# Two column tiles of a weight chunk on TensorE: one after the other in place of turn by turn

## What is computed

```python
h = rms_norm(x, norm_mix)
proj = h @ w_in                      # q, k, v, gates of both recurrences, merge gates
...
merged = sigmoid(ga) * (o_r @ w_ret_out) + sigmoid(gb) * (o_h @ w_hgrn_out)
x = x + merged @ w_out
g, u = split(rms_norm(x, norm_ffn) @ w_ffn_in)
x = x + (silu(g) * u) @ w_ffn_out
```

## Time and profile before

| what | value |
|---|---|
| median of three runs | 1765.47 us |
| the profiled execution | 1764.43 us, its span 1762.6 us |
| TensorE busy (matmul) | 1745.1 us, 14598 matmuls |
| VectorE, ScalarE, GpSimd busy | 1078.7, 766.9, 258.6 us |
| DMA | 334.11 MB, mean 190 GB/s |
| granted TensorE clock, mean | 0.996 of full speed |

### The profile page before, as it was taken

How to read it: one execution, slowest core, us unless ns; L and a number is a source line. 1 busy time by engine, 2 the same in 40 slices (tenths; PEclk the granted TensorE clock), 3 DMA queues, 4 the chain that set the end, 5 groups by cost and what they waited for, 6 DMA issues and landing times.

```text
span 1762.6 us, 37793 instructions
## 1 busy us (share of the span) xinstructions
PE 1745.1 (99%) x14598; PEld 1727.5 (98%) x14598; DVE 1078.7 (61%) x1290; ACT 766.9 (44%) x915; POOL 258.6 (15%) x378
## 2 busy tenths in 40 slices
PE   9899999999999999999999999999999999999997
PEld 9899999999999999999999999999999999999997
DVE  7776776766767755555566655555555555545444
ACT  7354454554554643444433444443444434333332
POOL 0561642733715000000000000000000000000000
PEclk9999999999999999999999999999999999999999
DMA  9566666676666555555566565565555655555553
GB/s 311 178 214 196 193 206 202 184 216 187 207 203 188 181 180 182 187 181 183 182 207 204 174 194 180 179 184 183 180 180 178 190 179 183 185 181 180 188 184 109
DMA packets 390169, 334.11 MB, mean 190 GB/s; under 512 B 12640, under 2 KB 387680, under 8 KB 390112
## 3 DMA queue, kind: packets, MB, share of 16 engines
q1 hardware_dynamic: 369968, 318.58, 58.6%
q10 hardware_dynamic: 20144, 14.72, 2.7%
HBM read 316.93 MB, written 16.32 MB: 189 GB/s over the span
## 4 chain that ended last, share of the span: by engine, by line
PE 97%; DVE 1%; DMA 1%; ACT 0%; issue 0%; DVEq 0%; SPq 0%; ACTq 0%
PE pA L1168 15%; PE pA L1170 15%; PE pA L1169 15%; PE pB L1168 13%; PE pB L1170 13%; PE pB L1169 13%; PE p L1168 3%; PE p L1170 3%; PE p L1169 3%; DMA raw<-in_w_in 1%; PE p L1288 1%; PE p L1313 1%; PE p L1195 0%; PE p L1185 0%; PE p L1268 0%; PE p L1261 0%
## 5 line engine op out<-in xcount | busy, mean ns | idle before, releaser
L758 DVE TENSOR_TENSOR lo<-raw,hi 128x1024 fp32r<-128x1024 f32 x567 | 711.9, 1260 | 559.6 <-ACT hi L458 553.7
L458 ACT CAST hi<-raw 128x1024 fp32r<-128x1024 f32 x567 | 594.0, 1048 | 746.7 <-PE pA L1170 353.9
L1168 PE MATMUL pA<-h_hi,hi 128*128 128x264 f32 x1688 | 484.1, 287 | 0.2 <-DVE lo L758 0.2
L1170 PE MATMUL pA<-h_hi,lo 128*128 128x264 f32 x1688 | 477.9, 283 | 0.0
L1169 PE MATMUL pA<-h_lo,hi 128*128 128x264 f32 x1688 | 477.9, 283 | 0.0
L1168 PE MATMUL pB<-h_hi,hi 128*128 128x264 f32 x1472 | 420.0, 285 | 5.4 <-DVE lo L758 5.4
L1170 PE MATMUL pB<-h_hi,lo 128*128 128x264 f32 x1472 | 417.4, 284 | 0.0
L1169 PE MATMUL pB<-h_lo,hi 128*128 128x264 f32 x1472 | 417.4, 284 | 0.0
L1168 PEld LDWEIGHTS pA<-h_hi,hi 128*128 128x128 f32 x1688 | 317.4, 188 | 5.9 <-issue 5.1
L1169 PEld LDWEIGHTS pA<-h_lo,hi 128*128 128x128 f32 x1688 | 317.4, 188 | 0.2
L1170 PEld LDWEIGHTS pA<-h_hi,lo 128*128 128x128 f32 x1688 | 317.3, 188 | 0.0
(11 more groups left out here) (263 smaller groups left out, 2360.6 us busy)
## 6 DMA issues: line engine op xcount, KB each, us to landing
raw<-in_w_fin SPq DMA_DIRECT2D x176, 512.0 KB, 3.5
raw<-in_w_in SPq DMA_DIRECT2D x128, 512.0 KB, 4.0
raw<-in_w_in SPq DMA_DIRECT2D x190, 256.0 KB, 3.4
raw<-in_w_fout SPq DMA_DIRECT2D x88, 512.0 KB, 3.8
raw<-in_w_ret SPq DMA_DIRECT2D x32, 512.0 KB, 4.5
raw<-in_w_out SPq DMA_DIRECT2D x32, 512.0 KB, 4.7
S_ret<-in_s_ret SPq DMA_DIRECT2D x32, 256.0 KB, 3.9
out_ret_s<-S_ret ACTq DMA_DIRECT2D x8, 1024.0 KB, 4.8
```

What stands on the lines that cost most here:

```text
L458: copy(hi[s], raw[s]).then_inc(hi_done, 1)
L758: tt(lo[s], raw[s], hi[s].bitcast(F32), ALU.subtract).then_inc(split_done, 1)
L1168: mm(outs[t][:, ::-1], w_hi, a_hi[:, kt, ::-1], start=(kt == 0), stop=False)
L1170: last = mm(outs[t][:, ::-1], w_lo, a_hi[:, kt, ::-1], start=False, stop=(kt == CK * n - 1))
```

## The change

In `use_chunk` the order that only `in_turn` chunks had becomes the order of every chunk. The argument `in_turn` stays and still sets the additional semaphore.

```diff
@@ -1162,7 +1162,7 @@
                 pe.wait_ge(split_done, c + (RING + 1))
                 for q in range(2 * CK):
 
-                    t, j = (q // CK, q % CK) if in_turn else (q % 2, q // 2)
+                    t, j = q // CK, q % CK
                     kt = CK * i + j
                     w_hi, w_lo = hi[s][:, j, t * P:t * P + P], lo[s][:, j, t * P:t * P + P]
                     mm(outs[t][:, ::-1], w_hi, a_hi[:, kt, ::-1], start=(kt == 0), stop=False)
```

## The result

The kernel after takes 1768.16 us (median of 20 runs, 1767.67 to 1768.95), the kernel before 1765.38 (20 runs, 1764.27 to 1766.39). The ratio is 1.0018, with a 95% interval of 1.0011 to 1.0024: slower by 2.8 us, surely not zero, and under the 0.2% that was set as the bound of "no change". The forecast was 1769.3 with a range of 1765.0 to 1772.0. The profiled execution took 1767.85 us, 3.4 more than that of before, and its granted clock was 0.996 on the mean, as before.

The account below looks back on a forecast made before the run. The prediction took TensorE's pace of matmul starts as the bound. It added 0.3 us in the FFN's output and 3.5 us elsewhere, 3.8 us in all, for a median of 1769.3 us, range 1765.0 to 1772.0.

Parts of the forecast that it names:

- What bounds the kernel: TensorE's pace of starting matmuls, 2.8833 us a chunk, sets the time; buffers, the ring and DMAs don't.
- Chunks 1 to 11 are covered: Their loss, if under 5 us, disappears in TensorE's 5.4 us wait for VectorE before chunk 12.
- Step 1: Eight row tile changes a chunk instead of four: 3.3 ns more, 0.3 us over 80 chunks of the FFN's output.
- Step 2: At the bank change activations jump back to row tile 0: 5 ns; with row tile changes 7.5 ns in 468 chunks, 3.5 us.
- the second rival: Slow matmul starts in every first half of a chunk: 33 ns a chunk, 18 us, 1783.5; chance 0.12.
- The sum: 0.3 + 3.5 = 3.8 us more on TensorE, the critical path all through.
- No jump cost: Only the row tile changes cost, 3.3 ns in 548 chunks: 1.8 us, 1767.3; chance 0.30.
- A slow rhythm that stays: Slow starts seen in the first chunk fill every chunk's first half: 18 us, 1783.5; chance 0.12.
- Nothing: The order of matmuls has no effect, since TensorE's read ports are independent: 1765.5; chance 0.07.
- The bank change: Returning from second PSUM bank to first costs the 0.8 ns, so fewer returns gain 1.4 us: 1764.1; chance 0.03.

Follow-up runs that it names:

- addresses alone: Kernel after, but the two PSUM banks take turns every three matmuls as before; weights and tokens read in the new order: 1768.29 us, 1.0018 of before.
- banks alone: Kernel before, but a chunk's first twelve matmuls go to one bank, the next twelve to the other; reads in the old order: 1764.70 us, ratio 0.9998.
- weights alone: Kernel before with activations at 224 bytes (32 in the FFN's output) and only the weights read in the new order: 1766.76 us, 2.8833 us a chunk.

## Why the prediction was right, and where it was off

**What bounds the kernel**: right. TensorE is busy all through, nothing waits anew, and the buffers and queues had no part in the difference.

**Chunks 1 to 11 are covered**: right. Chunk 12 started where it had started. The text said that the wait would shrink by less than 0.1 us and it shrank by 0.4, and that all three waits would stay, and the one of 0.2 us went. The first chunks are not steady, and their own unevenness is larger than the effect.

**Step 1, row tile changes**: right in size, 3.3 ns a chunk. It is shown by the FFN's output (3.3 ns in 70 chunks), by all activations at 32 (2.8867), and at 160 (2.8867). It was read from seven in-turn chunks, out of 0.02 us with rows rounded to 0.01, which allowed 0 to 5 ns. That it came out at 3 was partly luck; the count, twice the changes at 0.8, was the better ground.

**Step 2, the jump back**: the mechanism and its place were right, and the size was a little off. The text had 7.5 ns a chunk in 468 chunks; 6.7 was measured, so 3.1 us and not 3.5. (As written, 7 x 0.8 + 5 - 3.3 is 7.3; 7.5 comes with the unrounded 0.83.) The term that was mis-sized is the 5 ns for the jump: the chunk as a whole leaves 6.7 + 3.3 - 7 x 0.83 = 4.2.

That it was near is in part luck, for the 288 against 283 it was taken from belongs to other matmuls. The range of 282 to 288 in the earlier trace rows is that of L1330; the late start behind 9.99 belongs to L1329 (128 ns to the next start). The 288 are the four L1330 rows of the first bank, from 8.28 on, with 127 ns to the next start each: the slow rhythm of the second rival. In the kernel after the jump is still there and the 288 are gone:

```profile
L1330 PE MATMUL pA<-h_lo,hi x8: 281/283/285, 8.5 to 11.0; 128*128 128x264 f32 x8
```

What the first chunk did tell rightly is the place, the first matmul of the second row tile behind the jump, and by the rounded rows a size of 0 to 10 ns.

**The sum**: 3.8 forecast, 3.4 between the two profiled executions, 2.8 between the medians. The last difference is in the choice of a single execution: the profiled one of before was 1.0 us under its median, that of after 0.3. By the medians alone, 2.8 lies halfway between the likeliest case (3.8) and *No jump cost* (1.8); the pace of 2.8900 us a chunk decides between them, and so do the medians of addresses alone (3.3 over before).

**The rivals.** *No jump cost* would have given 1.8 us; the kernel at 32 bytes is that case and measured 1.8 (1766.74 against 1764.95). *A slow rhythm that stays* did not come; where it had been before, it went. In the first chunk the first bank's eleven starts took 9.79 - 8.47 = 1.32 us in the kernel after, where the earlier trace rows had 1.35.

```profile
8.47 0.28 PE L1330 MATMUL pA<-h_lo,hi 128*128 128x264 f32 x1
...
9.79 0.28 PE L1329 MATMUL pA<-h_hi,hi 128*128 128x264 f32 x1
```

So the same function in the same order ran both ways, and there the order within the chunk doesn't decide. In the chunk after the L1288 matmuls of a head it does. The eleven starts of the earlier trace rows took 1.36 us before and 1.33 after:

```profile
143.63 0.28 PE L1169 MATMUL pA<-h_lo,hi 128*128 128x264 f32 x1
...
144.96 0.28 PE L1168 MATMUL pA<-h_hi,hi 128*128 128x264 f32 x1
```

The trace's starts give 1.351 to 1.352 us in heads 1 to 7 before and with banks alone, and 1.325 to 1.326 after and with addresses alone; from its start to the next chunk's this chunk went from 2.998 to 2.978 us in all eight heads. That is the opposite of what the rival expected (the new order would have nothing to end it), and worth only 0.2 us in the whole.

*Nothing.* The Trainium skill's rule (SBUF — State Buffer, "Who interferes with whom") is that TensorE's two read ports are independent and that only the port pair shared by VectorE and GpSimd causes contention. As a guide to time the measurements decide against it: with the same instructions a chunk took from 2.883 to 2.960 us by placement alone. That the two reads contend at a port is not shown by this either. *The bank change*: banks alone had no effect. The Trainium skill (TensorE: Matmul & The Clock Gate, "A second HAM failure mode: psum-queue depth-cycling") puts the loss of a kernel that cycles through banks down to a clock that falls and rises again between bursts. Here banks that switch every three matmuls go with busy 200.00 of 200.00 us and a granted clock of 1.00, so nothing of it is seen.

What stays open is the mechanism inside. The runs show that the order in which the tokens are walked costs (at 224 bytes all of it), that the distance to the weights' address and the direction count, and that the weights' own order costs nothing as long as the distances it makes are good ones. Why a step costs 0.83 ns, why the jump costs more than a step at 0, 192 and 224 and not at 32 and 160, and which read holds up which, they do not show.

## What to carry to other kernels

All of this was seen on one kind of stream: fp32r matmuls of 128x128 weights by 264 columns, each with its own weight load, 120 ns apart. When TensorE streams so without a gap, the order of matmuls still has a price of its own, from under one to some nanoseconds in each change of the moving tile: at a good distance let the streamed operand walk forward by even steps, use each tile for all matmuls that need it before going on, and don't go back. Placement is worth far more than order (up to 77 ns a chunk against 7): try the distance between the two operands' addresses first, and treat it and the order as one setting. And a trace that already holds a few cases of the new order is a good price list; measure the distance between starts over many tiles, not the durations, and check that a duration belongs to the matmul that you mean.

## What the runs showed of the hardware that was not expected

- The mean cost of a steady chunk is reproducible to a tenth of a nanosecond in 2883: 493.05 us for 171 chunks in the kernel before, in banks alone, in weights alone and in the order of before at 160 bytes.
- Reading 264 tokens forward in place of backward, and writing the bank forward with them, costs 1.7% (1794.17 against 1764.38).
- Which order is the better one turns with the distance: after is slower by 27 ns a chunk at 128 bytes and faster by 20 at 64. Forward, at 192, it is faster too.
- A step back by one row tile costs 5.8 ns at 192 bytes, a step forward 0.83.
- After the L1288 matmuls of a head the starts of the next chunk fall into a slow rhythm (1.352 us for eleven in place of 1.32) or hardly do (1.326), by the order in which the operands are read.
